# Value panels of the last part by block products, with its first head's keys and queries and the modulation turns in other places

## What is computed

```
mod   = silu(c_2) @ w_mod + b_mod            # modulation: shift, scale, gate, six sections of 1024
u     = rms_norm(x, gain) * (1 + scale) + shift
q,k,v,gates,out_gate = split(u @ w_gla)      # q,k: 4 heads x 128; v: 1024; out_gate: 1024
decay = log_sigmoid(u @ down @ up + bias) / 16       # rank 16, for two directions
# per head h, both directions, over chunks of 64 tokens:
o_h   = (q_h * exp(sums of decay)) . (k_h * exp(-sums)) masked @ v_h + (carried state of k, v)
y     = (rms_norm(o_h) * silu(out_gate)) @ w_gla_o
```

## Time and profile before

| | us |
|---|---|
| median of 3 runs | 2398.2 (2395.15 to 2399.6) |
| profiled execution, its own time | 2394.6 |
| span of its instructions | 2392.7 |
| TensorE busy | 2297.9 (96%) |
| VectorE busy | 1384.9 (58%) |
| ScalarE busy | 506.4 |
| GpSimd busy | 167.2 |
| mean granted TensorE clock | 0.992 |

### The profile page before, as it was taken

One profiled execution on the slowest core, in us unless ns is written; L12 is line 12 of the kernel. 1 busy time (PEld: TensorE's weight loads), 2 busy tenths in 40 slices (PEclk: granted clock), 3 DMA queues, 4 the chain that ended last, 5 costly groups with the idle time before them and its releaser, 6 DMA issues.

```text
span 2392.7 us, 29353 instructions
## 1 busy us (share of the span) xinstructions
PE 2297.9 (96%) x11814; PEld 1841.6 (77%) x11814; DVE 1384.9 (58%) x2538; ACT 506.4 (21%) x1088; POOL 167.2 (7%) x133
## 2 busy tenths in 40 slices
PE   7999999999999999999999999999999999898998
PEld 5888587899778876869997555588888864577987
DVE  5764334645647433377867666766565455546666
ACT  1222220100011223101112354322200033432200
POOL 0000000430000000023400000000000000000000
PEclk9999999999999999999999999999999999999999
DMA  9853438545475333665564302343333335134442
GB/s 392 327 212 106 158 137 303 178 166 189 174 282 212 106 129 136 217 241 193 186 225 140 137 2 71 115 135 130 124 141 106 114 125 200 46 117 174 165 152 79
DMA packets 163508, 391.31 MB, mean 164 GB/s; under 512 B 6448, under 2 KB 10928, under 8 KB 160560
## 3 DMA queue, kind: packets, MB, share of 16 engines
q1 hardware_dynamic: 136736, 285.03, 33.4%
q0 software_dynamic: 24080, 93.69, 10.9%
q10 hardware_dynamic: 2560, 10.72, 1.2%
HBM read 388.37 MB, written 1.05 MB: 163 GB/s over the span
## 4 chain that ended last, share of the span: by engine, by line
PE 88%; DVE 7%; ACT 2%; DMA 1%; issue 1%; SPq 0%; DVEq 0%; ACTq 0%
PE bank L535 86%; DVE arena L2017 3%; DVE arena L2023 2%; PE bank L533 2%; DMA arena<-in_w_ada 1%; ACT arena L1389 1%; ACT arena L1392 1%; DVE arena L2020 1%; DVE junk L2023 1%; DVE arena L2960 0%; ACT L1389 0%; DVE arena L2155 0%; DVE arena L2992 0%; DVE arena L2086 0%; SPq L3073 0%
## 5 line engine op out<-in xcount | busy, mean ns | idle before, releaser
L535 PE MATMUL bank<-arena 128*128 128x256 f32 (+3 forms) x11326 | 2241.3, 366 | 52.6 <-DVE arena L2017 19.8
L535 PEld LDWEIGHTS bank<-arena 128*128 128x128 f32 (+1 forms) x11326 | 1784.1, 190 | 497.1 <-issue 280.9
L2017 DVE TENSOR_TENSOR arena<-arena 128x1024 f32<-128x1024 f32 (+9 forms) x555 | 462.1, 846 | 243.3 <-PE bank L535 201.5
L1389 ACT ACTIVATE arena<-arena 128x512 f32<-128x512 f32 (+5 forms) x426 | 213.5, 522 | 812.0 <-DVE arena L2017 457.6
L2023 DVE SCALAR_TENSOR_TENSOR arena<-arena 128x1028 f32<-128x1028 f32 (+6 forms) x367 | 309.0, 858 | 122.5 <-DMA arena<-in_w_ada 87.8
L1392 ACT ACTIVATE arena<-bank 128x512 f32<-128x512 f32 (+1 forms) x207 | 115.3, 595 | 490.0 <-PE bank L535 450.0
L2017 DVE TENSOR_TENSOR arena<-arena,bank 128x256 f32<-128x256 f32 (+2 forms) x312 | 140.8, 476 | 133.8 <-PE bank L535 125.2
L3127 POOL DMA_DIRECT2D arena<-in_w_ada x88 | 62.7, 712 | 1897.4 <-DVEq L2032 1886.8
L2017 DVE TENSOR_TENSOR arena<-bank,arena 128x512 f32<-128x512 f32 (+3 forms) x103 | 69.7, 690 | 215.2 <-PE bank L535 196.2
L1389 ACT ACTIVATE arena<-bank 128x256 f32<-128x256 f32 (+2 forms) x119 | 49.0, 430 | 500.5 <-PE bank L535 499.8
L2023 DVE SCALAR_TENSOR_TENSOR arena<-bank,arena 128x254 f32<-128x254 f32 (+2 forms) x184 | 78.1, 469 | 50.9 <-PE bank L533 34.7
(11 more groups left out here) (33 smaller groups left out, 168.4 us busy)
## 6 DMA issues: line engine op xcount, KB each, us to landing
arena<-in_w_ada POOLq DMA_DIRECT2D x88, 1028.0 KB, 5.5
arena<-in_w_in SPq DMA_DIRECT2D x84, 1024.0 KB, 7.3
arena<-in_w SPq DMA_DIRECT2D x56, 1024.0 KB, 6.0
arena<-in_w_mlp_in SPq DMA_DIRECT2D x32, 1024.0 KB, 6.5
arena<-in_w_mlp_out SPq DMA_DIRECT2D x32, 1024.0 KB, 6.6
arena<-in_w_gla SPq DMA_DIRECT2D x12, 1024.0 KB, 7.3
arena<-in_w_ada SPq DMA_DIRECT2D x16, 514.0 KB, 19.4
arena<-in_w_a SPq DMA_DIRECT2D x8, 1024.0 KB, 6.6
```

Of the source, the lines that this page charges most:

```text
L535: ins = nc.tensor.matmul(out, lhsT, rhs, start=start, stop=stop)
L1389: return nc.scalar.activation(out, x, f, **kw)
L2017: return V.tensor_tensor(out, x, y, op)
```

## The change

- The value panels are computed as seven block products each, `gv(p, i)`, in the order 1, 2, 5, 7, 6, 4, 3 for panel 0 and 1, 2, 4, 5, 7, 6, 3 for panel 1. A product has 2 x 4 matmuls: 128 tokens by 128 rows as the stationary side, 256 columns as the moving side. The rank projection comes after product 2 of panel 0, the decay tiles after products 5 and 6.
- VectorE makes four token sums once (`token_sums`, 128 x 1024 each), weight sums w6 and w3 for each panel (128 x 1024), and for each panel one first sum and six product sums (128 x 512). GpSimd makes w5 and w7 of both panels (`value_sums`, 128 x 1024), ahead of modulation panels 74 and 78, with semaphore `gv_sums_made`. ScalarE evicts only product 1 of each panel.
- `gk(0)` and `gq(0)` stand ahead of the last three products of panel 1. That panel's buffers are released behind these.
- Of the twelve turns, nine stay ahead of `products_of(0)`, in other places; three go into the head loop, behind `magnitudes(h + 2)` of heads 0, 1 and 2. Panel 1's product sums, but for the first, stand behind `products_of(0)`.

Cut to its core:

```diff
+        gv_x = [UT2[:, KH * j:KH * j + KH, T * n:T * n + T] for j in range(2) for n in range(2)]
+        gv_sums = {i: area(at, KH, T) for i, at in ((5, G0 + 1024), (6, G0 + 8192), (7, g1 + 2816), (4, g1 + 3840))}
...
-            for p in range(2):
-                w = panel()
-                for tt in range(4):
-                    token_tile(f"GV {p} {tt}", w, tt, UT2)
-                    if (p, tt) == (0, 0):
...
-                    elif p == 0 and tt in (1, 3):
-                        gz_(tt // 2)
-                release(w)
+            def gv(p, i):
+
+                a11, a12, a21, a22 = quarters(gv_panel(p))
+                w, x = {1: (a11, gv_x[0]), 2: (a12, gv_x[2]), 4: (a22, gv_sums[4]), 5: (wsum, gv_sums[5]),
+                        7: (a21, gv_sums[7]), 6: (a11, gv_sums[6]), 3: (a12, gv_x[3])}[i]
+                ps = open_tile(f"GV {p} {i}")
+                if i in (4, 5, 6, 7):
+                    pe.wait_ge(dve_done, DV.at(f"GV x{i}"))
+                if i in (5, 7):
+                    pe.wait_ge(gv_sums_made, 2 * p + (1 if i == 5 else 2))
+                if i in (6, 3):
+                    pe.wait_ge(dve_done, DV.at(f"GV {p} w{i}"))
+                for u in range(2):
+                    for k in range(KH):
+                        mm(ps[:, u * T:u * T + T], x[:, k, u * P:u * P + P], w[:, k, :], start=(k == 0), stop=(k == KH - 1),
+                           done=f"GV {p} {i}" if u and k == KH - 1 else None)
+
+            w = panel()
+            gv(0, 1)
+            gv(0, 2)
+            evicted("next", range(2, 4))
...
+            gv(0, 5)
+            gz_(0)
+            gv(0, 7)
+            gv(0, 6)
+            gz_(1)
+            gv(0, 4)
+            st["held"].add(marks.get((Progress.phase, "bank", "GV 0 5"), 0))
+            gv(0, 3)
+            st["held"].clear()
+            release(w)
+            wv = panel()
+            for i in (1, 2, 4, 5):
+                gv(1, i)
             wk, wq = panel(), panel()
...
             gk(0)
             gq(0)
+            for i in (7, 6, 3):
+                gv(1, i)
+            release(wv)
...
                 if h == 0:
                     for p in range(2):
-                        for tt in range(4):
-                            pe.wait_ge(act_done, AC.at(f"GV {p} {tt} drained"))
+                        pe.wait_ge(dve_done, DV.at(f"GV {p} c12"))
...
-            for n, q in enumerate(ADA_LATER[:12]):
+            turns = iter(ADA_LATER[:12])
+
+            def gla_turn():
+
+                q = next(turns)
                 ada_turn(q, [("ada", 1)])
                 if q == 11:
                     gate("g1")
-                if n in (2, 4):
-                    magnitudes(n // 2 - 1)
-                    decays(n // 2 - 1)
+
+            dve.wait_ge(act_done, AC.at("next 3 0 drained"))
+            token_sums("GV", gv_x, [gv_sums[i] for i in (5, 6, 4)], False, gv_sums[7])
+            value_sum(0, 6)
+            value_sum(0, 3)
+            first_sum("GV 0", gv_blocks(0), value_read(0))
+            gla_turn()
+            gla_turn()
+            magnitudes(0)
+            gla_turn()
+            gla_turn()
+            decays(0)
+            values = product_sums("GV 0", gv_blocks(0), value_read(0))
+            next(values)
+            next(values)
+            magnitudes(1)
+            gla_turn()
+            next(values, None)
+            value_sum(1, 6)
+            decays(1)
             arguments(0)
+            value_sum(1, 3)
+            first_sum("GV 1", gv_blocks(1), value_read(1))
+            for n in range(4):
+                gla_turn()
             products_of(0)
+            for _ in product_sums("GV 1", gv_blocks(1), value_read(1)):
+                pass
...
                 if h + 2 < G_HEADS:
                     magnitudes(h + 2)
+                if h < G_HEADS - 1:
+                    gla_turn()
...
+            def value_sums(p):
+
+                a11, a12, a21, a22 = quarters(gv_panel(p))
+                for m in range(gv_panel(p), gv_panel(p) + 2):
+                    pool.wait_ge(panel_in[m % RING], 16 * (m // RING + 1))
+                if p:
+                    pool.wait_ge(pe_of["gla"], PE.of("gla", "GV 0 5 full"))
+                    pool.wait_ge(dve_of["gla"], DV.of("gla", "GV 0 w6"))
+                else:
+                    pool.wait_ge(pe_of["attn"], PE.of("attn", "end"))
+                    pool.wait_ge(dve_of["attn"], DV.of("attn", "end"))
+                nc.gpsimd.tensor_tensor(wsum, a21, a22, ALU.add).then_inc(gv_sums_made, 1)
+                pool.wait_ge(gv_sums_made, 2 * p + 1)
+                nc.gpsimd.tensor_tensor(a21, a11, a21, ALU.subtract).then_inc(gv_sums_made, 1)
+
             for n, (job, q) in enumerate(jobs + [(DEPTH + 1, q) for q in ADA_LATER]):
 
+                if n in (74, 78):
+                    value_sums((n - 74) // 4)
```

More of the change, by code:

```diff
@@ L269, in program @@
         c_in = [sem(f"c{i}_in") for i in range(2)]
[L270 removed]
+        up_sums_made, gv_sums_made = sem("up_sums_made"), sem("gv_sums_made")
         masks_in, first_free = sem("masks_in"), sem("first_free")
@@ L405, in program, with gv_blocks, gv_panel @@
         gdec = area(sm + 160, 2, 8)
+        gv_x = [UT2[:, KH * j:KH * j + KH, T * n:T * n + T] for j in range(2) for n in range(2)]
+        gv_sums = {i: area(at, KH, T) for i, at in ((5, G0 + 1024), (6, G0 + 8192), (7, g1 + 2816), (4, g1 + 3840))}
+        def gv_blocks(p):
+            return {(i, m): gV[:, 2 * m - 2:2 * m, PW * p + 2 * P * (i - 1):PW * p + 2 * P * i] for i in (1, 2) for m in (1, 2)}
+        def gv_panel(p):
+            return first_of[0, "w_gla"] + 2 + 2 * p
         def aux(at):
@@ L441, in program @@
         first_of = {(l, w): min(n for n, j in enumerate(half_panels()) if j[:2] == (l, w))
-                    for l in range(2) for w in ("w_mlp_in", "w_mlp_out", "w1", "w2")}
+                    for l in range(2) for w in ("w_mlp_in", "w_mlp_out", "w1", "w2", "w_gla") if l == 0 or w != "w_gla"}
         def quarters(n, kh=KH):
@@ new lines, in _ @@
+            w = panel()
+            gv(0, 1)
+            gv(0, 2)
+            evicted("next", range(2, 4))
+            ps = open_tile("DN")
+            pe.wait_ge(ranks_in, 16)
+            for k in range(KD):
+                mm(ps[:64, :], w_down[:, k, :], UT2[:, k, :], start=(k == 0), stop=(k == KD - 1),
+                   done="DN" if k == KD - 1 else None)
+            gv(0, 5)
[5 more added lines that the diff above has]
+            st["held"].add(marks.get((Progress.phase, "bank", "GV 0 5"), 0))
@@ L1939, in _, with first_value @@
                 modulated2("next", tt, 0)
[L1940 to L1949, removed]
+            def first_value(p):
+                act.wait_ge(pe_done, PE.at(f"GV {p} 1 full"))
+                func(gv_blocks(p)[1, 2], tile(f"GV {p} 1").rearrange("p (a b) -> p a b", a=2), ACT.Copy).then_inc(
+                    act_done, AC.drained(f"GV {p} 1"))
+            first_value(0)
+            act.wait_ge(pe_done, PE.at("DN full"))
+            func(gDT[:64, :], tile("DN")[:64, :], ACT.Copy).then_inc(act_done, AC.drained("DN"))
+            for h in range(2):
+                biased(h)
+                decays(h)
+            first_value(1)
             def gk(h):
@@ L3001, in products_of, with value_sum, value_read @@
                         dve_done, DV.step(f"gprep {h}" if e else None))
-            for n, q in enumerate(ADA_LATER[:12]):
+            def value_sum(p, i):
+                if i == 6:
+                    dve.wait_ge(gv_sums_made, 2 * p + 2)
+                panel_sums(f"GV {p}", gv_panel(p), i, f"GV {p} {1 if i == 6 else 2}")
+            def value_read(p):
+                return lambda i: tile(f"GV {p} {i}").rearrange("p (a b) -> p a b", a=2)
+            turns = iter(ADA_LATER[:12])
+            def gla_turn():
+                q = next(turns)
                 ada_turn(q, [("ada", 1)])
```

## The result

| | before | after |
|---|---|---|
| median (us) | 2398.2 | 2382.88 |
| lowest to highest (us) | 2395.15 to 2399.6 | 2378.07 to 2385.66 |
| ratio to before, 95% interval | | 0.9939 (0.9928 to 0.995) |
| profiled execution, its span (us) | 2394.6, 2392.7 | 2382.88, 2381.1 |

What follows compares the result with a forecast made beforehand. TensorE's streaming and waiting was taken to bound the kernel. 6.6 + 5.2 + 2.6 - 0.3 = 14.1 us took the profiled 2394.6 to 2380.5 us, 2384.1 us against the median; range 2379.5 to 2391.

Steps and rivals of the forecast that it cites:

- What bounds the kernel: Whole kernel: TensorE carries 88% of the chain that ended last, so less streaming or less waiting there shortens it.
- Part 1: Value panels on TensorE: seven products for eight save 3.28 us a panel, 6.6 us in all.
- The rival in which seven products take the time of eight: Value panels: no hidden weight load, so only parts 2 and 3 gain, about 7.5 us: 2390.7 us; chance 0.05.
- Part 2: Ahead of head 0: VectorE is ready before TensorE arrives at 2035.5 us, so the 5.2 us wait goes.
- the walk: VectorE's new list followed in time up to head 0: gprep 0 at about 2027 us, at the latest 2032.
- Part 3: Head 0: without the gap ahead of it the clock doesn't fall, so 2.6 us come back; bounds 0 and 3.0.
- Part 4: Head loop: three turns of 2.5 us mostly fit into waits and cost 0.3 us; bounds 0 and 7.5.
- 0.83 + 1.94 us, nothing: Head 3 in the loop: waits of 0.83 and 1.94 us take up the turn, so it costs nothing.
- Part 5: GpSimd's sums, later buffer releases, banks and ScalarE's evictions: all counted at nothing.
- The turns landed on the chain: Head loop rival: all three turns cost in full, 7.5 for 0.3 us, leaving 6.9 us: 2391.3 us; chance 0.12.
- The clock fell: Rival: the clock falls anyway or a value-panel product stalls, leaving 9 to 11.5 us: 2387 to 2389 us; chance 0.17.
- The slower rival: Ahead of gprep 0: VectorE's list sets head 0's start and its additions simply add: 2406.3 us; chance 0.04.

Runs made afterwards that it cites:

- the last experiment: The changed kernel with GpSimd's w5 and w7 sums of panel 1 left out, so that panel's values are wrong: 2383.93 us, ratio 0.9951 to before.
- filled wait: The kernel before plus six unread matmuls of 512 columns ahead of TensorE's wait for gprep 0: 2393.77 us, ratio 0.9985.
- x5: The changed kernel with the head loop's three turns moved between arguments(h + 1) and products_of(h + 1): 2379.45 us, ratio 0.9939 to before.
- x4: The changed kernel with only the three loop turns put back ahead of products_of(0), seven in a row there: 2398.79 us, ratio 1.0005 to before.

## Why the prediction was right, and where it wasn't

**What bounds the kernel.** Right. The wait, the streaming and the clock each moved the end by what was read off the trace before.

**Part 1** (6.6 us): 6.75 us less streaming to head 0, with no wait inside the value panels, so the pace of a product was indeed that of the second MLP's output stage. The rival in which seven products take the time of eight is out.

**Part 2** (5.2 us): right. In before's frame head 0 starts at 2038.35 - 3.03 = 2035.3 us, where 2035.5 stood; gprep 0 is there at 2032.4 - 3.03 = 2029.4, between the 2027 and the 2032 of the walk. What the walk had priced only as a bound was VectorE standing still beside GpSimd: 4.1 us were really lost, on the scans and not on the sums of 128x1024. The prediction held that most of VectorE's list there wasn't two-input work of that size, and so took 0; that step was wrong about VectorE and right about TensorE, as the last experiment shows. The Trainium skill (SBUF — State Buffer, Who interferes with whom) says that VectorE work with two inputs in SBUF and GpSimd work that reads SBUF hold each other off; the scan's 6.41 for 2.34 us is this case's number for it. The ends fit too: the two scans end at 1997.28, 1.1 us behind GpSimd's second sum (1993.04 + 3.14 = 1996.18), and one scan lasts 1.17 us.

**Part 3** (2.6 us): right, 2.58 us in the changed kernel. The filled wait shows it apart from all else, 2.5 us with head 0 starting at the same moment. The premise, that without a gap the clock has no reason to fall, held in head 0 of every profile that has no wait there over 0.5 us. It isn't true everywhere: the last section has a fall without a gap.

**Part 4** (0.3 us): the term that was mis-sized. The waits that the turns add on TensorE are 0.45 us ahead of head 2 (3.23 us for 2.78; 3 was forecast) and 0.68 us ahead of the burst: 1.1 us, which x5 takes back. The step that failed was head 3's "0.83 + 1.94 us, nothing": the turn made TensorE wait 1.31 us for 0.63 ahead of the burst. The walk also didn't follow the clock, and the clock decides more there than the turns do. From head 1 to the burst the kernel before takes 54.41 us, the changed one 54.81, x5 52.41, and the filled kernel, with no turn in the loop, 52.41 too. Before's clock fell at head 2 and, behind a gap of 3.11 us, at head 3; after's fell at head 2 for longer and, behind 2.77 us at head 3, not at all: 8.39 us became 7.43. So these rows sum to -0.40, against -0.3, by errors of opposite sign. The sum's agreement to 0.1 us is in part luck.

**Part 5** (nothing): right in the total, with the 4.1 us above hidden. The rest of the program behind the burst took 267.0 us for 267.5.

**The rivals.** The turns landed on the chain with 1.1 us of waits, of their 7.5 us; with the clock behind them, 2.4 at most. The clock fell at head 2 as before. The slower rival's mechanism is real, and this is the most useful thing that the runs show: put all turns ahead of head 0, as in x4, and VectorE's list sets the start (13.60 us of wait), taking the whole gain of the products; it still wasn't measurably slower than before (ratio 1.0005). The rival's bound (from over 8 us of lateness on, slower only past 20) agrees: x4's head 0 is 1.8 us later than before's from the gate tile (92.42 for 90.63), which is 2049.1 in before's frame and 22 us behind the walk's 2027, and its burst is 0.24 us later. What kept it from happening was that four turns, not seven, stand ahead.

**The median.** From the profiled execution the sum gave 2380.5 us and the shift to the median 2384.1. The profiled execution of after took 2382.88. The 2.4 us between are the 3.03 us by which it entered the stage late, less 0.5 us behind the burst. Those 3.03 us are the clock in stages that no edit touches (last section); without them the profiled execution would lie about 3 us lower. How much of such a loss the other four executions had isn't known, so the 1.2 us between forecast and median are in part luck.

## What to carry to other kernels

A saving on the bound engine pays only if the list that it waits for next gets shorter too: here seven products for eight gave nothing with the turns left where they were, 14 us with three of them moved. Work that only has to be done sometime belongs where its engine waits for *another* one (1.1 us of waits here for three turns, and 1.3 us of clock that went with them), and the bound engine should wait for the earlier of two results first (another 4.6 us of the stage). Where a wait can't be closed, price the clock behind it as well, and try keeping TensorE busy through it.

## What the hardware did that was not expected

**The clock behind the same gap.** In unchanged code at the end of the attention stage TensorE waits 3.67 us in both kernels and then does the same 32 transposes. Before, then after:

```profile
1934.39 6.46 PE L535 MATMUL bank<-arena 128*128 128x128 f32 x32 [3.67 <-issue]
```

```profile
1940.06 3.81 PE L545 MATMUL bank<-arena 128*128 128x128 f32 x32 [3.67 <-issue]
```

Before, the granted clock fell to 0.50 (1.2 GHz) and in after it stayed at 1.00: 2.65 us that no edit explains. A gap of 2.78 us at head 2 was followed by half clock, one of 2.77 us at head 3 wasn't.

**Why the changed kernel entered the stage late.** It reached those 32 transposes 5.67 us behind the kernel before, and made up 2.65 us there: 3.02 us are left. The 5.67 us were lost in stages that no edit touches. From 650 to 660, 710 to 720 and 1190 to 1200 us its mean granted clock is 0.83, 0.66 and 0.83, and 1.00 in the kernel before. That is 1.7, 3.4 and 1.7 us at these means, 6.8 in all, less the 0.9 us by which it was ahead at 650. The first and the third stand behind gaps of 3.06 and 2.50 us, which before has as well. The second has no gap: TensorE is busy without a break from 661.54 on, and the clock is at half from about 712.8 to 719.6:

```profile
714.00:716.00 2.00, 2.00 (x6) 1.64 (x6) 0.45 (x3) 1.41 (x2) 0.00 (x0) 0.50 0.22 84
```

The clock fell at this place in seven of the twelve profiles and stayed at 1.00 in five. What makes it fall there, no run shows. Across the twelve profiles the stage's zero lies between 1956.66 and 1962.09 us, 5.4 us apart, for the same code ahead of it. Whoever compares two traces by their absolute times reads this as an effect of the change.

**Useless work that pays.** Six unread matmuls in a wait of 5.2 us made the kernel 3.5 us faster by the medians.

**GpSimd's sums and VectorE's scans.** Two scans of 128x512 took 6.41 us beside two GpSimd sums of 128x1024, and 2.34 us without; the GpSimd sum took 3.14 us at its slowest there.
